# Mixture of experts: the down product of a step moved behind the next step's first products, two result buffers, separate waits for gate and up weights

## The reference, cut to what matters

```python
order = jnp.argsort(flat_e)                       # tokens sorted by expert
buf = zeros(...).at[dest].set(xf[tok_sorted])     # each expert's tokens start a new block
block_e = ...                                     # the expert of each block

def expert_block(args):
    xb, e = args
    hb = jax.nn.silu(xb @ w_gate[e]) * (xb @ w_up[e])     # w_gate, w_up: 1024 x 512
    return hb @ w_down[e]                                 # w_down: 512 x 1024

y = lax.map(expert_block, (buf, block_e))
out = zeros(...).at[tok_sorted].add(y[dest] * w_sorted[:, None])
```

## Time and profile before

| | us |
|---|---|
| median of three runs | 6976.05 (6958.89 to 6981.98) |
| the profiled execution | 6989.38 |
| its span, first to last instruction | 6987.6 |
| TensorE busy in the span | 5603.2 (80%) |
| VectorE, ScalarE, GpSimd busy | 2333.7, 1178.4, 301.6 |
| gate products, stages moe1 and moe0 (L1183) | 178.9 and 173.2 busy |
| up products, each stage (L1183) | 169.0 busy |
| down products, moe0 and moe1 (L1202) | 181.6 and 178.6 busy |
| VectorE writing y, moe0 (L1268) | 36.0 busy, 460.1 idle before it, 443.4 of it ended by the store of y |

### The profile page before, as it was taken

The page is one execution under the profiler, slowest core; times in us unless marked ns, Lnnn a source line. Parts: engine busy times, 40 slices in busy tenths (PEclk is TensorE's granted clock), DMA queues, the critical chain, the costliest instruction groups (busy, mean ns, idle before and its releaser), DMA issues. The chain is left out here.

```text
span 6987.6 us, 96082 instructions
## 1 busy us (share of the span) xinstructions
PE 5603.2 (80%) x39658; PEld 3068.0 (44%) x39658; DVE 2333.7 (33%) x3925; ACT 1178.4 (17%) x1918; POOL 301.6 (4%) x320
## 2 busy tenths in 40 slices
PE   7998858894986548688859989889558998867778
PEld 4554443332456425233334338888524444322233
DVE  2334310003205643100045365555442120443331
ACT  1222100001110020000023122222201110422111
POOL 0000000001010000000010000000000000211100
PEclk9998869996998757799969999999879999889989
DMA  2110155553133330654332243232231222467721
GB/s 103 36 36 31 60 200 203 220 199 129 48 110 102 111 120 26 244 218 184 146 100 84 80 135 67 53 70 53 73 114 39 57 71 82 145 228 260 254 103 63
DMA packets 559787, 813.87 MB, mean 116 GB/s; under 512 B 176648, under 2 KB 308104, under 8 KB 558920
## 3 DMA queue, kind: packets, MB, share of 16 engines
q1 hardware_dynamic: 491272, 629.25, 27.0%
q0 software_dynamic: 28544, 103.82, 4.2%
q10 hardware_dynamic: 39616, 75.51, 3.0%
HBM read 967.67 MB, written 209.26 MB: 168 GB/s over the span
## 5 line engine op out<-in xcount | busy, mean ns | idle before, releaser
L701 PE MATMUL op_acc<-op_w,op_m 128*128 128x512 f32 x1024 | 451.1, 601 | 63.1 <-DMA op_w<-in_w_out 63.1
L158 PE MATMUL hi_acc<-xT,hi_w 128*128 128x512 f32 x1024 | 445.6, 594 | 8.0 <-DMA hi_w<-in_odd_w_in 8.0
L701 PEld LDWEIGHTS op_acc<-op_w,op_m 128*128 128x128 f32 x1024 | 196.1, 193 | 304.8 <-issue 240.1
L158 PEld LDWEIGHTS hi_acc<-xT,hi_w 128*128 128x128 f32 x1024 | 193.4, 191 | 242.4 <-issue 234.1
L158 PE MATMUL ri_acc<-xT,ri_w 128*128 128x512 f32 (+1 forms) x576 | 253.8, 599 | 10.6 <-DMA ri_w<-in_even_w_in 10.6
L537 PE MATMUL na_acc<-xT,na_w 128*128 128x512 f32 x448 | 219.5, 638 | 40.0 <-DMA na_w<-in_na_w_in 34.0
L158 PE MATMUL di_acc<-xT,di_w 128*128 128x512 f32 x512 | 224.8, 598 | 8.4 <-DMA di_w<-in_even_w_in 8.4
L158 PE MATMUL mi_acc<-xT,mi_w 128*96 128x512 f32 (+1 forms) x512 | 224.3, 598 | 0.0
L3483 PE MATMUL le_gp<-le_g,xT 128*128 128x512 f32 x512 | 220.9, 592 | 0.0
L1183 PE MATMUL moe1e_g_ps<-moe1e_wg,moe1e_xb 128*64 128x512 f32 x768 | 178.9, 620 | 32.9 <-DMA moe1e_wu<-in_exp_w_up 25.7
L1183 PE MATMUL moe0e_g_ps<-moe0e_wg,moe0e_xb 128*64 128x512 f32 x768 | 173.2, 604 | 22.8 <-DMA moe0e_wu<-in_exp_w_up 15.3
(11 more groups left out here) (669 smaller groups left out, 8944.5 us busy)
## 6 DMA issues: line engine op xcount, KB each, us to landing
moe0e_wg<-in_exp_w_gate SPq DMA_DIRECT2D x48, 2048.0 KB
moe0e_wu<-in_exp_w_up SPq DMA_DIRECT2D x48, 2048.0 KB
moe0e_wd<-in_exp_w_down SPq DMA_DIRECT2D x48, 2048.0 KB
moe1e_wg<-in_exp_w_gate SPq DMA_DIRECT2D x48, 2048.0 KB
moe1e_wu<-in_exp_w_up SPq DMA_DIRECT2D x48, 2048.0 KB
moe1e_wd<-in_exp_w_down SPq DMA_DIRECT2D x48, 2048.0 KB
op_m<-scratch_mixedT SPq DMA_DIRECT2D x32, 512.0 KB, 8.8
op_w<-in_w_out SPq DMA_DIRECT2D x32, 512.0 KB, 9.9
```

The lines of the kernel that those rows point to most:

```text
L158: mm = pe.matmul(self.acc[i % 2][0:n, h * BANK:(h + 1) * BANK], self.wbuf[i % 3][:, k, 0:n], self.rhs[:, k, h * BANK:(h + 1) * BANK], star ...
L701: mm = pe.matmul(acc[:, n % AHEAD, h * BANK:(h + 1) * BANK], m[:, k, n * P:(n + 1) * P], wb[:, k, h * BANK:(h + 1) * BANK], start=(k == 0) ...
```

## The change

One buffer pair `hy` takes the place of `h` and `y`: its half 0 is y's half 0, and its half 1 is both `h` and y's half 1. Each half has its own semaphore for the store. On TensorE the down product of a step is cut into two parts of 8 products and issued in the next step: gate and up products, transposes of x part 0, down of the step before part 0, transposes of x part 1, down part 1, transposes of h. The last step's down product stands by itself at the end. Gate and up weights have a semaphore each, waited for ahead of the gate and of the up products; SyncE issues the gate loads of both streams ahead of the up loads, and all first gate and up loads ahead of the first down loads. Its loop is shifted to match the later down product. ScalarE issues both stores of a step behind the copy of the next step's `hT`, copies x part 0 ahead of Silu, and Silu waits for the store of half 1 of the step before the last. VectorE writes both halves of y behind each other, the second after h has been turned. The core of the diff (definitions that only change names are left out):

```diff
-        h = s.sb("h", [P, F])
         hT = s.sb("hT", [P, KF, P])
-        y = s.sb("y", [P, BANK])
+        hy = s.sb("hy", [P, H, BANK])
+        assert H == 2 and F == BANK
+        y, h = [hy[:, q, :] for q in range(H)], hy[:, 1, :]
...
+                def load_in(which, experts, new):
+                    for w, source, loaded in ((wg, w_gate, gate_loaded), (wu, w_up, up_loaded)):
+                        for l, b in enumerate(which):
+                            only = {} if new is None else {"cond": new[l]}
+                            sp.dma_start(w[b][:], source.rearrange("e (k p) f -> e p k f", p=P)[experts[l]], **only).then_inc(loaded[b], 16)
+                def load_down(which, experts, new):
+                    for l, b in enumerate(which):
+                        only = {} if new is None else {"cond": new[l]}
+                        sp.dma_start(wd[b][:], w_down.rearrange("e (k p) f -> e p k f", p=P)[experts[l]], **only).then_inc(down_loaded[b], 16)
+                def coming(table, b, most, first, i):
+                    later = table[0:1, b * TURNS + first + 1:(b + 1) * TURNS].rearrange("p (t a) -> p t a", a=1)
+                    return sp.value_load(later[:, 0 if i is None else i, :], min_val=0, max_val=most)
+                def next_in(first, i, c):
+                    experts = [coming(expert, b, E - 1, first, i) for b in streams(c)]
+                    new = [coming(fresh, b, 1, first, i) for b in streams(c)]
+                    sp.wait_ge(ups, count(first, i, 2, c + 1))
+                    load_in(streams(c), experts, new)
+                def next_down(first, i, c):
+                    experts = [coming(expert, b, E - 1, first, i) for b in streams(c)]
+                    new = [coming(fresh, b, 1, first, i) for b in streams(c)]
+                    sp.wait_ge(results, count(first, i, 2, c + 1))
+                    load_down(streams(c), experts, new)
...
+                begin = [[sp.value_load(expert[0:1, b * TURNS:b * TURNS + 1], min_val=0, max_val=E - 1) for b in streams(c)] for c in range(2)]
+                for load in (load_in, load_down):
                     for c in range(2):
-                        def coming(table, b, most):
-                            later = table[0:1, b * TURNS + 1:(b + 1) * TURNS].rearrange("p (t a) -> p t a", a=1)
-                            return sp.value_load(later[:, i, :], min_val=0, max_val=most)
-                        e = [coming(expert, b, E - 1) for b in streams(c)]
-                        new = [coming(fresh, b, 1) for b in streams(c)]
-                        sp.wait_ge(ups, i * 2 + (c + 1))
-                        for l, b in enumerate(streams(c)):
-                            load_in(b, e[l], cond=new[l])
-                        sp.wait_ge(results, i * 2 + (c + 1))
-                        for l, b in enumerate(streams(c)):
-                            load_down(b, e[l], cond=new[l])
+                        load(streams(c), begin[c], None)
+                next_in(0, None, 0)
+                next_in(0, None, 1)
+                next_down(0, None, 0)
+                with sp.Fori(0, TURNS - 2) as i:
+                    next_in(1, i, 0)
+                    next_down(0, i, 1)
+                    next_in(1, i, 1)
+                    next_down(1, i, 0)
+                next_down(TURNS - 2, None, 1)
...
                 def hide(first, i, c):
-                    for b in streams(c):
-                        pe.wait_ge(in_loaded[b], count(first, i, 32, 32))
                     pe.wait_ge(x_kept, count(first, i, 4, 2 * c + 2))
-                    for ps, w, used, sem in ((g_ps, wg, gated, gates), (u_ps, wu, h_made, ups)):
+                    for ps, w, loaded, used, sem in ((g_ps, wg, gate_loaded, gated, gates), (u_ps, wu, up_loaded, h_made, ups)):
+                        for b in streams(c):
+                            pe.wait_ge(loaded[b], count(first, i, 16, 16))
                         pe.wait_ge(used, count(first, i, 2, c))
...
-                def down(first, i, c):
-                    for b in streams(c):
-                        pe.wait_ge(down_loaded[b], count(first, i, 16, 16))
-                    pe.wait_ge(hT_kept, count(first, i, 2, c + 1))
-                    if first:
-                        pe.wait_ge(y_kept, count(first, i, 2 * H, c * H - H))
-                    for k in range(KF):
+                def down(first, i, c, part):
+                    if part == 0:
+                        for b in streams(c):
+                            pe.wait_ge(down_loaded[b], count(first, i, 16, 16))
+                        pe.wait_ge(hT_kept, count(first, i, 2, c + 1))
+                        if first:
+                            pe.wait_ge(y_kept, count(first, i, 2 * H, c * H - H))
+                    for k in range(part * KF // 2, (part + 1) * KF // 2):
                         for q in range(H):
                             for l, b in enumerate(streams(c)):
                                 mm = pe.matmul(y_ps[half[l], c, q * BANK:(q + 1) * BANK], hT[:, k, half[l]], wd[b][:, k, q * BANK:(q + 1) * BANK],
                                                start=(k == 0), stop=(k == KF - 1))
-                    mm.then_inc(results, 1)
+                    if part == 1:
+                        mm.then_inc(results, 1)
                 def turn(first, i):
                     for c in range(2):
                         more = c == 0 or first < TURNS - 1
                         following = (first, i, 1) if c == 0 else (first + 1, i, 0)
+                        before = (first, i, 0) if c == 1 else (first - 1, i, 1)
                         hide(first, i, c)
-                        if more:
-                            turn_x(*following, 0)
+                        for part in range(2):
+                            if more:
+                                turn_x(*following, part)
+                            if c == 1 or first > 0:
+                                down(*before, part)
                         turn_hidden(first, i, c)
-                        if more:
-                            turn_x(*following, 1)
-                        down(first, i, c)
                 turn_x(0, None, 0, 0)
                 turn_x(0, None, 0, 1)
                 all_turns(pe, turn)
+                for part in range(2):
+                    down(TURNS - 1, None, 1, part)
...
-                def store(first, i, c, q):
-                    act.wait_ge(y_kept, count(first, i, 2 * H, c * H + q + 1))
-                    of_turn = y_rows.rearrange("(l c i p) (q d) -> c q i l p d", l=2, c=2, p=SLOTS, q=H)[c, q, first:]
-                    act.dma_start(of_turn[0 if i is None else i], y[:]).then_inc(y_stored, 16)
+                def store(first, i, c):
+                    of_step = y_rows.rearrange("(l c i p) (q d) -> c q i l p d", l=2, c=2, p=SLOTS, q=H)[c]
+                    for q in range(H):
+                        act.wait_ge(y_kept, count(first, i, 2 * H, c * H + q + 1))
+                        act.dma_start(of_step[q, first:][0 if i is None else i], y[q]).then_inc(y_stored[q], 16)
                 def turn(first, i):
...
                         more = c == 0 or first < TURNS - 1
                         following = (first, i, 1) if c == 0 else (first + 1, i, 0)
                         before = (first, i, 0) if c == 1 else (first - 1, i, 1)
-                        some = c == 1 or first > 0
-                        if some:
-                            store(*before, 0)
+                        if more:
+                            keep_x(*following, 0)
                         act.wait_ge(gates, count(first, i, 2, c + 1))
                         act.wait_ge(h_turned, count(first, i, 2, c))
-                        act.activation(h[:], g_ps[:], ACT.Silu).then_inc(gated, 1)
+                        if first:
+                            act.wait_ge(y_stored[1], count(first, i, 32, 16 * c - 16))
+                        act.activation(h, g_ps[:], ACT.Silu).then_inc(gated, 1)
                         if more:
-                            keep_x(*following, 0)
+                            keep_x(*following, 1)
                         act.wait_ge(h_turned, count(first, i, 2, c + 1))
                         act.wait_ge(results, count(first, i, 2, c))
                         act.activation(hT[:], h_ps[:], ACT.Copy).then_inc(hT_kept, 1)
-                        if more:
-                            keep_x(*following, 1)
-                        if some:
-                            store(*before, 1)
+                        if c == 1 or first > 0:
+                            store(*before)
                 for part in range(2):
                     keep_x(0, None, 0, part)
                 all_turns(act, turn)
+                store(TURNS - 1, None, 1)
                 for q in range(H):
-                    store(TURNS - 1, None, 1, q)
-                act.wait_ge(y_stored, 16 * 2 * H * TURNS)
```

(66 more changed lines are left out.)

## The result

The changed kernel takes 6894.51 us (median of 4 runs, 6875.49 to 6915.86) against 6979.01 for the kernel before on the same chip (4 runs): ratio 0.9885, 95% interval [0.985, 0.992]. The forecast was 6909 with a range of 6855 to 6955.

A forecast was written before the change was run, and what follows sets the result against it. TensorE was busy but stalled by two y stores per step chained through one buffer, on two saturated DMA engines. Order -29.4, start -31.3, tail +19.6, stalls -25.4 sum to -66.5 off the 6976 median: 6909 us, range 6855 to 6955.

The forecast's parts named there:

- the step of 22.5: TensorE, both stages: an undisturbed step takes 22.5 us between gate starts instead of 23.2, with no wait in it.
- Start: Start of each stage: products follow their weights, so step 2 begins 15.6 us earlier per stage, -31.3 us for two.
- Order: TensorE's order of products and transposes: two short waits go, added changes cost some; 42 x 0.7 = -29.4 us.
- Stalls: Waits on y stores in both stages: losses of 109 us instead of 134.6, so -25.4 us.
- the opening of the first stage: First stage's early steps, loads behind steps 1, 2, 2, 3 after the initial ones: 34 us of losses.
- the pairs of loads: Weight loads behind two successive steps: a pair of stores lands late, stall 2.4 us, 4.1 with slow clock.
- the slow clock behind a stall: TensorE runs at a lower clock for a while after a stall: 1.7 to 2.9 us added.
- the stretch with two streams at once and a third behind: Second stage, weights of two streams loaded together with a third load behind them: 15 us lost.
- Tail: Last gate product to the next stage's first issue: four stores in a row on two engines, +9.8 per stage, +19.6 us.
- Gate and up waited for apart: Mid-stage, beyond the start: the second stage's 10.3 us of later weight waits, inside the losses, counted as gone.
- the first (slower through the shared half): Silu waits for the second of two stores; fully loaded steps take 32 us, +33 us, 7009 us; chance 0.11.
- The second (no stalls at all): Two queued stores' slack always suffices, stores stop stalling; some 25 us remain for weights, 6825 us; chance 0.09.

The follow-up runs named there:

- experiment 4: Changed kernel with up weights again waited for ahead of gate products and first loads in the old order: 6916.03 us, 0.9911 of the kernel before.
- experiment 7: Kernel before with gate and up weights waited for apart and first loads in the new order: 6998.81 us, ratio 1.0027.
- Experiment 9: Changed kernel with each y store cut into one transfer per lane and the down product in one piece: 6801.38 us, 0.9746 of the kernel before.
- Experiment 1: Changed kernel with each y store cut into two transfers of 64 partitions, one per lane: 6787.33 us, 0.9722 of the kernel before.
- experiment 3: Changed kernel with y's halves weighed and stored in the other order, the half shared with h first: 6833.99 us, 0.979 of the kernel before.
- experiment 5: Changed kernel with each y store cut in two by columns, lanes still the outer dimension: 6931.49 us, 0.9929 of the kernel before.
- experiment 2: Kernel before, single y buffer, with each y store cut into two transfers of 64 partitions, one per lane: 6834.3 us, ratio 0.9786.

## Why the prediction was right, and where its sizes were off

The time lies 15 us below the forecast and inside the range, and the mechanisms of its four terms show in the trace. That the number came so close is in part luck: over the two profiled stages the change is -99.7 where -66.5 was forecast, and three of four terms were mis-sized by about half. The order of the products was given 13 us too much; the stalls were given 32 and the tail 10.5 us too little. Two of the signs that the prediction named didn't come: the step of 22.5 (22.8), and no stall of 7 us or more outside the first opening (the longest is 10.2).

- **Start, -31.3, measured -34.7.** Right, and experiments 4 and 7 show that it needs both edits: the new loads without the later down product lose 5.8 and 7.2 us at step 2, the later down product without them loses 16 against the changed kernel and is then about where the kernel before was (83.2 and 83.6 against 84.3).
- **Order, "six changes of 0.07", -29.4, measured -16.4.** The waits of 0.27 and 0.43 went as forecast. The change between products and transposes costs 0.12, not 0.07: 20.6 + 3 x 0.49 + 6 x 0.12 = 22.8. Experiment 9 bears it out: it has four changes instead of six and is 0.23 shorter without its wait. The 0.1 per change stood in the same rows, and I went below it without a row; the earlier trace rows even hold one for the other direction, 1199.48 - 1198.45 less the wait of 0.43, which is 0.60 or 0.11 more than 0.49. The prediction also speaks of two added changes where there are four (two before, six after); its sum counts the six.
- **Stalls, 109 left, measured 76.8.** The mechanism was right: Silu behind the second store of a pair on two engines (experiments 1, 3 and 5 show each part). Too large were the opening of the first stage, forecast at 34 and measured at 19.7 (from step 2 to 7, 133.8 less five steps), that of the second (13, measured 6.6), the pairs of loads (4.1 each, measured 1.7 for those behind steps 12 and 20) and the slow clock behind a stall: up to 2.9, measured 1.6 after a stall of 4.59 and 2.1 after one of 6.23 (the gate product behind takes 8.25 and 8.74 instead of 7.09, the slow transposes are in it). Behind the stall of 6.23 the granted clock is 0.50 of full speed from 1251.5 to 1254.5 and 1.00 again from 1256.5, as in the undisturbed step. Behind the pairs the slow clock didn't come at all: their stalls are 1.64 and 1.61 instead of 2.4, and the transposes of h after them take 0.66. Too small was the stretch with two streams at once and a third behind, 15 against 20.6, where the longest stall is 10.2. A pair of stores needs 11.7 us alone instead of the 12.7 of two lone ones, which gives every pair a microsecond more of slack; with an earlier issue its last packet ends 13.0 us into the step (1144.7 - 1131.72), where 1.75 + 12.7 = 14.5 was forecast.
- **Tail, +19.6, measured +9.1,** in part for the same reason: four stores in a row took 21.9 us, not 25.4, and none of the 1.6 us of slow clock came (the last down product takes 7.09). The two make 5.1 of the 5.3 us per stage.
- **Gate and up waited for apart** was counted as a gain in mid-stage, inside the stalls' term; experiment 7 shows that by itself it gives none.

Of the rivals, the first (slower through the shared half) had the right mechanism: the shared half is what still stalls. It needed 29.9 us per step in the 707.9 us of weights; the longest steps reached 35.37, but few. The second (no stalls at all) did not come with this change, whose losses are still 76.8. Experiment 1 shows a kernel without stalls, at 6787 rather than 6825: the 25 us that I had kept for late weights weren't needed, and its tail is 12.0 shorter than before where the rival has +19.6, while the order gives 13 less.

What I didn't ask is whether the two engines could be left: the prediction read the 12.8% as given and walked its consequences for four terms. What stays open is why the profiled spans differ by 114.0 and the medians by 84.5. Of the gap of 29.5, 14.3 lies outside the stages; the other 15 may lie in either part, which single profiles can't tell. In eight of the nine experiments the change of the stages and that of the median, both against the kernel before, agree within 7 us (experiment 9: 14).

## What to carry to other kernels

Before buffers are doubled to hide a slow store, ask how many DMA engines it takes: its share in the queue row, times 16, against the outer dimension of its pattern. Here cutting the store along that dimension was worth 96 us of the stages in the changed kernel and 153 in the one before, where the whole change was worth 100, and it made the second buffer nearly superfluous. Where a buffer is shared by two uses, the one that is wanted first goes out first (52 us of the stages in experiment 3). And an early start counts only if nothing later in the in-order queue waits for what now comes last (experiment 7).

## What the hardware showed that I had not expected

Two stores in a row with two engines' share take less than twice a lone one, 11.7 against 2 x 6.4 us. A transfer on two engines can also delay loads that use all 16: in the kernel before, weights came 10.3 us late in the second stage behind its start, and in experiment 2, which differs only in the pattern of the stores, none came late behind step 2, although the same bytes moved in less time. And the part of the span that no edit touches varied by 25 us between profiled executions, more than a quarter of this change.
